# Half-turned keys and queries by transfers instead of matmuls, sums of squares in two parts, and four reorderings, in a two-block transformer kernel on one core

## The reference

```python
proj = einsum('btd,dn->btn', rmsnorm(h), w_in)
(gq, gk, gv, gz, gb, ga, aq, ak, av, iq, ik, iw, gate_a, gate_b) = split(proj)
# gated delta rule (GDN): q and k divided by their norms, per head of 128
q, k = _l2norm(q) * 128 ** -0.5, _l2norm(k)
# attention: 8 query heads aq, 2 key heads ak of 128, rotary position code
def _apply_rope(x, cos, sin):
    x1, x2 = x[..., :half], x[..., half:]
    return concatenate([x1 * c - x2 * s, x2 * c + x1 * s])
# index scores choose the keys that a query sees
s = einsum('bqhd,bsd->bqhs', qi, ki); s = einsum(relu(s), wi); top_k(s)
y_dsa = softmax(q k / sqrt(128), over the chosen keys) @ v
merged = sigmoid(gate_a) * (y_gdn @ w_a) + sigmoid(gate_b) * (y_dsa @ w_b)
```

## Time and profile before

| what | value |
|---|---|
| median of 3 runs | 1268.47 us (1268.13 to 1269.49) |
| profiled execution, its own time | 1269.95 us |
| its span | 1268.2 us |
| mean granted clock of PE | 0.998 |
| PE busy | 1254.3 us, 99% of the span |
| DVE, ACT, POOL busy | 919.6, 699.2, 154.3 us |

### The profile page before, as it was taken

How to read it: one execution, slowest core, us unless ns; L and a number is a source line. 1 busy time by engine, 2 the same in 40 slices (tenths; PEclk the granted TensorE clock), 3 DMA queues, 4 the chain that set the end, 5 groups by cost and what they waited for, 6 DMA issues and landing times.

```text
span 1268.2 us, 23324 instructions
## 1 busy us (share of the span) xinstructions
PE 1254.3 (99%) x9041; PEld 1169.6 (92%) x9041; DVE 919.6 (73%) x1290; ACT 699.2 (55%) x1082; POOL 154.3 (12%) x113
## 2 busy tenths in 40 slices
PE   9999999999999999999999999999999999999998
PEld 8997999999989998889998989999889998999986
DVE  6886874878778774447734547999758777999954
ACT  5556465654456343345354546666547567766642
POOL 0000142000000000000000001642200000464310
PEclk9999999999999999999999999999999999999999
DMA  7552332322355555555553444555564444454562
GB/s 300 189 173 101 133 134 101 133 68 68 152 197 188 195 179 185 198 170 182 183 209 109 156 173 167 198 169 195 194 221 171 162 154 163 167 188 175 197 224 93
DMA packets 30315, 212.83 MB, mean 168 GB/s; under 512 B 3488, under 2 KB 3616, under 8 KB 5152
## 3 DMA queue, kind: packets, MB, share of 16 engines
q1 hardware_dynamic: 29088, 206.53, 46.9%
q0 software_dynamic: 1152, 5.24, 1.1%
HBM read 210.71 MB, written 1.05 MB: 167 GB/s over the span
## 4 chain that ended last, share of the span: by engine, by line
PE 86%; DVE 8%; ACT 4%; DMA 1%; issue 1%; SPq 0%; DVEq 0%; ACTq 0%
PE lin L540 50%; PE lin L702 21%; DVE wlo L513 3%; PE lin L2883 2%; PE lin L567 2%; ACT whi L506 2%; PE lin L569 1%; DMA raw<-in_stream 1%; PE aux L2627 1%; PE aux L2599 1%; PE aux L2485 1%; ACT lm L1377 1%; PE aux L725 1%; PE aux L2745 1%; PE aux L2555 1%
## 5 line engine op out<-in xcount | busy, mean ns | idle before, releaser
L513 DVE TENSOR_TENSOR wlo<-raw,whi 128x2048 fp32r<-128x2048 f32 x183 | 427.4, 2338 | 170.8 <-ACT whi L506 170.1
L506 ACT CAST whi<-raw 128x2048 fp32r<-128x2048 f32 x192 | 365.3, 1906 | 179.5 <-DMA raw<-in_stream 147.0
L540 PE MATMUL lin<-xhi,whi 128*128 128x256 f32 (+2 forms) x1616 | 461.5, 286 | 1.0 <-DVE wlo L513 1.0
L540 PE MATMUL lin<-xlo,whi 128*128 128x256 f32 (+2 forms) x1616 | 457.0, 283 | 0.0
L540 PE MATMUL lin<-xhi,wlo 128*128 128x256 f32 (+2 forms) x1616 | 454.7, 281 | 0.0
L540 PEld LDWEIGHTS lin<-xhi,whi 128*128 128x128 f32 x1616 | 304.1, 188 | 3.0 <-DVE wlo L513 1.2
L540 PEld LDWEIGHTS lin<-xhi,wlo 128*128 128x128 f32 x1616 | 306.1, 189 | 0.0
L540 PEld LDWEIGHTS lin<-xlo,whi 128*128 128x128 f32 x1616 | 304.6, 189 | 0.4
L865 POOL TENSOR_TENSOR fu<-fs,ft 128x256 f32<-128x256 f32 x44 | 86.2, 1958 | 259.4 <-ACT fs L1479 259.4
L2292 DVE SCALAR_TENSOR_TENSOR ft<-fy,par,ft 128x254 f32<-128x254 f32 (+1 forms) x176 | 109.5, 661 | 5.9 <-DVE ft L2292 0.2
L540 PE MATMUL lin<-whi,xhi 128*128 128x256 f32 x256 | 74.2, 290 | 0.0
(11 more groups left out here) (454 smaller groups left out, 2123.2 us busy)
## 6 DMA issues: line engine op xcount, KB each, us to landing
raw<-in_stream SPq DMA_DIRECT2D x193, 1024.0 KB, 4.9
gp<-in_gains POOLq DMA_DIRECT2D x6, 512.0 KB, 3.9
c<-in_const SPq DMA_DIRECT2D x1, 1460.0 KB, 16.0
h<-in_x SPq DMA_DIRECT2D x2, 544.0 KB, 4.4
c<-in_const POOLq DMA_DIRECT2D x1, 1024.0 KB, 6.5
ht<-in_xtok POOLq DMA_DIRECT2D x1, 1024.0 KB, 9.6
out<-ht SPq DMA_DIRECT2D x1, 512.0 KB, 2.6
out<-ht SPq DMA_DIRECT2D x2, 256.0 KB, 2.0
```

The costliest lines, as they stand in the source:

```text
L506: nc.scalar.copy(whi[:, s0 % 4], raw[:, s0 % 4]).then_inc(hi_ready, 1)
L513: nc.vector.tensor_tensor(wlo[:, s0 % 4], raw[:, s0 % 4], whi[:, s0 % 4].bitcast(F32), ALU.subtract).then_inc(lo_ready, 1)
L540: ins = nc.tensor.matmul(out, a, b, start=start and n == 0, stop=stop and n == 2)
```

## The change

1. The matmuls that turned ak and aq go, and the constant `turna` with them. ACT waits for its own copy of ak or aq out of PSUM, then issues two transfers (`exchange`), one for each half of the partitions, that write the exchanged halves to new buffers `akr` and `aqr`: ten transfers of 64 partitions. The sign is now in the constant of the sines. DVE waits for both transfers (32) and does three operations as before, all from SBUF.
2. The table has another order. The sums of squares are cut into 5 and 11 matmuls with the index scores (0, 1) between; `sel` and `cum` come later, the decays' sums on DVE (`decay_sums`) go from `top(0)` into `top(1)`, two low halves on DVE come later. The second half of a tile's index scores uses the three banks that `l2sum` or `cum` doesn't hold. PE waits for rotations 7, 8 and 9 apart.
3. The cast of the third slot comes between the second and the third piece of `act_high_mix`.
4. Two parts of the branch projection (12 matmuls of 128 x 128) come ahead of a level of the GDN's first chunk; the decayed queries of the second chunk are made in two halves of four heads.
5. The very last tile is multiplied by its gains in one operation of 512 columns and gets two residuals of 512 in place of four pieces.

```diff
...
-PROJECT = [("rot", 0), ("iq", 0), ("iq", 1), ("rot", 1), ("rot", 2), ("av", 0), ("idx", 0, 0), ("lo", "aq", 1), ("l2", 0),
-           ("l2t", 0), ("sel", 0), ("idx", 0, 1), ("ak", 0), ("avt", 0), ("top", 0), ("cum", 0), ("idx", 1, 0), ("lo", "aq", 2), ("rot", 3), ("rot", 4),
+PROJECT = [("rot", 0), ("iq", 0), ("iq", 1), ("rot", 1), ("rot", 2), ("av", 0), ("idx", 0, 0), ("lo", "aq", 0),
+           ("l2", 0), ("idx", 0, 1), ("lo", "aq", 1), ("l2", 1), ("l2t", 0), ("ak", 0), ("avt", 0), ("top", 0),
+           ("sel", 0), ("idx", 1, 0), ("cum", 0), ("lo", "aq", 2), ("rot", 3), ("rot", 4),
...
-        ROT = ["rot_ik", "rot_iq0", "rot_iq1", "rot_ak0", "rot_ak1"] + [f"rot_aq{n}" for n in range(4)]
+        ROT = ["rot_ik", "rot_iq0", "rot_iq1"]
...
             if step[0] == "rot":
-                use_next(ROT[step[1]])
+                if step[1] < 3:
+                    use_next(ROT[step[1]])
+            elif step[0] == "idx" and step[2]:
+                others = [b for b in range(4) if b != USE[("l2sum", "cum")[step[1]]][0]]
+                for hh in range(4, 8):
+                    use(others[hh % 3], f"idx{step[1]}_{hh}")
...
                 use_next("avt0", "avt1")
-            elif step[0] in ("l2", "l2t", "sel", "cum"):
+            elif step[0] in ("l2t", "sel", "cum") or step == ("l2", 0):
                 use_next({"l2": "l2sum"}.get(step[0], step[0]))
-        use_next(ROT[8])
...
                 a = slice(n * 512, n * 512 + 512)
-                sp.wait_ge(S("h_postffn1"), 7 + 2 * n)
+                sp.wait_ge(S("h_postffn1"), 5 + n)
...
             for c in range(4):
+                if c == 2:
+                    load_hi(2, 0)
...
             act_high_mix(act)
-            load_hi(2, 0)
...
+            def exchange(dst, src, name):
...
+                for lo in (0, 64):
+                    act.dma_start(dst[lo:lo + 64], src[64 - lo:P - lo]).then_inc(S(name), 16)
...
                     nc.scalar.copy(ak[:], PS[u % 2][:, :, 0:T1]).then_inc(pair_free[u % 2], 1)
+                    pair_done(act, u)
+                    exchange(akr[:], ak[:], "swap_ak")
...
                     nc.scalar.copy(dst[:, 2 * j:2 * j + 2], PS[u % 2][:, :, META:T1]).then_inc(pair_free[u % 2], 1)
+                    if name == "aq":
+                        pair_done(act, u)
+                        exchange(aqr[:, 2 * j:2 * j + 2], aq[:, 2 * j:2 * j + 2], f"swap_aq{j}")
...
                     is_free(nc.scalar.copy(av[0:META, 2], b[0:META, 0:NCOL]), "avt1")
-                elif step[0] == "l2":
+                elif step[0] == "cum":
+                    act.wait_ge(S("bcg"), 1)
+                    own.link(nc.scalar.activation(kroot, knorm, ACT.Sqrt))
+                elif step == ("l2", 1):
...
                 elif step[0] in STEP_SLOTS:
-                    if step[0] == "ak":
-                        act.wait_ge(S("bcg"), 1)
-                        own.link(nc.scalar.activation(kroot, knorm, ACT.Sqrt))
...
             def second_tile(u):
+                if not pre:
+                    own.link(gained(u, 1, 0, 512, 512))
+                    dve.wait_ge(S("root_" + tag), 2)
+                    own.link(nc.vector.reciprocal(rc[:, 1:2], rc[:, 1:2]))
+                    residual(1, 0, 512)
+                    residual(1, 512, D)
+                    return
...
                 n = x.shape[1]
+                if step > 2:
+                    dve.wait_ge(S("swap_ak" if step < 5 else f"swap_aq{step - 5}"), 32)
+                    nc.vector.tensor_tensor(name, name, bc(cst(sn, lo=t0, n=W), n), ALU.mult)
+                    own.link(nc.vector.tensor_tensor(x, x, bc(cst(c, lo=t0, n=W), n), ALU.mult))
+                    nc.vector.tensor_tensor(x, x, name, ALU.add).then_inc(S("rope"), 1)
+                    dve.wait_ge(S("rope"), step + 1)
+                    return
...
             for step in PROJECT:
-                if step[0] == "iq":
-                    load_lo(FIRST["iq"] + step[1] + 3, 0)
+                if step == ("iq", 0):
+                    load_lo(FIRST["ak"], 0)
...
                 elif step[0] == "top":
-                    top_bias(step[1], between=None if step[1] else decay_sums)
+                    top_bias(step[1], between=decay_sums if step[1] else None)
...
                 own.link(nc.vector.tensor_tensor(dms[s][:, a], dms[s][:, a], gain, ALU.mult))
+                if between:
+                    between()
...
-            def decayed_queries(s):
-                q = qkv[:, 0:8, META + (s - 1) * P:META + s * P]
-                nc.vector.tensor_tensor(q, q, eg[:], ALU.mult).then_inc(S("ke"), 1)
+            def decayed_queries(s, h0, h1):
+                q = qkv[:, h0:h1, META + (s - 1) * P:META + s * P]
+                nc.vector.tensor_tensor(q, q, eg[:, h0:h1], ALU.mult).then_inc(S("ke"), 1)
...
             triangles(2, 0)
-            triangles(2, 1)
+            triangles(2, 1, lambda: decayed_queries(2, 0, 4))
...
             blocks(2)
+            decayed_queries(2, 4, H1)
             new_state(1)
-            decayed_queries(2)
-            dve.wait_ge(S("ke"), 2)
+            dve.wait_ge(S("ke"), 3)
...
             for n in range(2):
-                yield f"rot_ak{n}", ak[:, n:n + 1], T1, "cosa", "sina", 0
+                yield akr[:, n:n + 1], ak[:, n:n + 1], T1, "cosa", "sina", 0
             for n in range(4):
-                yield f"rot_aq{n}", aq[:, 2 * n:2 * n + 2], SEQ, "cosa", "sina", META
+                yield aqr[:, 2 * n:2 * n + 2], aq[:, 2 * n:2 * n + 2], SEQ, "cosa", "sina", META
...
                 name, x, W, c, sn, t0 = todo[step]
-                turn = cst("turni" if c == "cosi" else "turna")
+                turn = cst("turni")
...
                     pair_done(pe, 0)
-                elif name[:6] == "rot_iq":
+                else:
                     pair_done(pe, pair_first["iq"] + int(name[6:]))
-                elif name[:6] == "rot_ak":
-                    pair_done(pe, pair_first["ak"])
-                else:
-                    pair_done(pe, pair_first["aq"] + int(name[6:]))
...
                 if step[0] == "rot":
-                    rotation(step[1])
+                    if step[1] < 3:
+                        rotation(step[1])
...
                 elif step[0] == "l2":
-                    pe_head_sums(pe)
+                    pe_head_sums(pe, step[1])
...
                     project(step[0], step[1])
-            gate_part(0, 0, 2)
-            rotation(8)
-            gate_part(0, 2, 5)
-            pe.wait_ge(S("rope"), 9)
+            gate_part(0, 0, 5)
+            pe.wait_ge(S("rope"), 7)
...
             gate_part(0, 5, 6)
+            pe.wait_ge(S("rope"), 8)
...
             gate_part(0, 6, 7)
+            pe.wait_ge(S("rope"), 9)
...
             read_state(1, 1)
+            pe.wait_ge(S("slo"), 2)
+            branch(0, 0, 2)
...
                 additions(g)
-            pe.wait_ge(S("slo"), 2)
-            branch(0, 0, 3)
+            branch(0, 2, 3)
...
-        def pe_head_sums(pe):
...
-            b = fill("l2sum")
-            pe.wait_ge(S("l2sq"), 2)
-            for n in (*range(8, 16), *range(8)):
+        def pe_head_sums(pe, part):
...
+            if part == 0:
+                pe.wait_ge(S("l2sq"), 2)
+            b = AUX[USE["l2sum"][0]] if part else fill("l2sum")
+            for n in (*range(13, 16), *range(8)) if part else range(8, 13):
...
                 ins = nc.tensor.matmul(b[0:16, t0:T1], c1[:, a:a + 16], src[:, n % 8, t0:T1], start=n == 8, stop=n == 7)
-            is_full(ins, "l2sum")
+            if part:
+                is_full(ins, "l2sum")
...
```

More of the change, by code:

```diff
@@ L214, in program @@
         irelu = at("irelu", B + 74112, [P, 4, T1])
+        akr = at("akr", B + 67584, [P, 2, T1])
+        aqr = at("aqr", B + 82560, [P, 8, SEQ])
         zs = at("zs", B + 76288, [P, 8, SEQ])
@@ L3019, in constants @@
         c["cos" + tag], c["sin" + tag] = np.cos(ang), np.sin(ang)
-        turn = np.zeros((P, P), f)
-        for m in range(P):
-            lo = m % dim < dim // 2
-            turn[m + dim // 2 if lo else m - dim // 2, m] = -1.0 if lo else 1.0
-        c["turn" + tag] = turn
+    c["sina"] = np.where((i < 64)[:, None], -c["sina"], c["sina"])
+    c["turni"] = np.zeros((P, P), f)
+    for m in range(P):
+        lo = m % 64 < 32
+        c["turni"][m + 32 if lo else m - 32, m] = -1.0 if lo else 1.0
     past = [np.where(pos[None, :] <= (META + t * P + i)[:, None], 0.0, -BIG) for t in range(2)]
```

9 lines of the change are left out of this document (4 added, 5 removed).

## The result

The changed kernel takes 1277.32 us (median of 4 runs, 1275.17 to 1279.27), the kernel before in the same measurement 1268.3 (1267.64 to 1269.49): **slower by 0.7%, ratio 1.0071 with an interval of 1.0059 to 1.0083**. Forecast were 1265.2 us and a range up to 1268.2. The profiled execution is the fastest of the four: 1275.17 us, span 1273.0.

A forecast was written before the change was run, and what follows sets the result against it. PE, busy 99% of the span, was taken as the bound. Gains of 0.5 (attention, after the clock fall), 1.0 (start), 1.2 (GDN) and 0.45 (end) summed to 3.15, giving 1265.2 us; range 1262.4 to 1268.2.

The forecast's parts named there:

- the last exchange: Transfer for the last aq pair: assumed to land 3.0 us after its second issue, at 160.6, last rotation ending at 162.8.
- a late landing as a rival: Slower: last exchange lands after 9.6 us, attention loses 4.7, total 1270.5 us; deciding from a landing near 7.5. Chance 0.08.
- +1.9: Attention stage: last rotation's end, and what follows it, 1.9 us earlier if PE keeps its clock.
- I take 1.4: Slot aq 1, behind the new 3.0 us wait: a clock fall, held more likely than not, costing 1.4 us.
- the prediction's own signs of being wrong: Exchanges over 7 us, relu free without the cast ahead, or clock falling where the earlier trace shows none.
- the term of 1.75 us for the fall in `ak`: Slot ak: cutting the 16-column matmuls removes the clock fall, gaining 1.75 us; called the least certain gain, bounds 0 and 1.75.
- The start, GDN and end: Gains outside attention: 1.0 us from the third slot's cast, 1.2 from the branch matmuls, 0.45 from the last tile.
- The new wait of 3.0 us for ACT's relu: Behind aq 0: fourth matmul of index scores (1, 1) waits for its bank behind copy, issues, cast and relu; 3.0 us.
- the wait of 0.8 behind `ak`: Behind ak: ACT issues two transfers before copying avt out, so PE newly waits 0.8 us for banks.
- ACT is held for its issues as SP is: ACT's queue: 0.95 us taken for two issues with the copy's end, from SP's 0.90 for two; lower bound zero.
- Slot `ak` at 6.0: Slot ak takes 6.0 us at a clock of 1.00, in place of 7.76.
- the transfer and not DVE would be late next: Last rotation: DVE's own earliest end near 162.0, so the transfer is late next, by 0.8 us.

The follow-up runs named there:

- experiment 5: Changed kernel, but SP issues the weight slot freed by an ak or aq slot only once that slot's exchange has landed: 1273.29 us, ratio 1.0042.
- Experiment 6: Changed kernel with one transfer of 128 partitions in place of two of 64, halves not exchanged, so computation is left out: 1271.4 us, ratio 1.0032.
- Experiments 7: Changed kernel, but ACT casts the high part of the slot behind aq 0 after the relus of index scores (1, 1): 1272.4 us, ratio 1.0042.
- 9: Changed kernel plus 19 unread matmuls, 7 in the wait at index scores (1, 1) and 12 at the logits: 1272.76 us, ratio 1.0036.
- 10: Changed kernel plus only the 7 unread matmuls in the wait at index scores (1, 1): 1271.53 us, ratio 1.0033.
- 12: Kernel before with items 3, 4 and 5 of the change, plus three banks for index scores (1, 1), no exchange: 1269.01 us, ratio 1.0004.
- Experiment 15: Kernel before with items 3, 4 and 5, plus the sums of squares cut into 5 and 11 around index scores (0, 1): 1265.91 us, ratio 0.9984.
- experiments 8: Changed kernel, but the last pair of aq (rotation 9) is turned by a matmul as before: 1272.78 us, ratio 1.0026.
- 14: Kernel before with items 3, 4 and 5, plus the two DVE low halves moved behind the index scores: 1267.21 us, ratio 0.9992.
- 11: Changed kernel plus only the 12 unread matmuls in the wait at the logits: 1275.63 us, ratio 1.0057.

## Why the prediction was wrong

**The step that failed** is the last exchange, "I take 3.0, between 2.0 and 4.9, and nearer the row of the like size". It landed after 6.7 us, the others after 5.5 to 6.2. I went by the size; what counts is the weight slot issued within a us ahead of it (experiment 5). The row of the weight slot, 4.9, was taken as the upper bound and lies below every landing in the trace; the weight slots beside the exchanges took 5.8 themselves. Experiment 6 shows that even 256 KB take the same. That the two share the engines and the one issued second lands last is my reading of these rows. The prediction had a late landing as a rival, at a chance of 0.08. With the measured landing its own sum gives 4.88 - 6.7, or -1.8 us for the attention stage in place of +1.9, and with the other terms as they stand a kernel 0.5 us slower than before (-1.8 - 1.4 + 2.65), 1269 us. So this step alone does not explain the 1277.3.

Without a slot beside it the exchange took 2.2 to 2.4 us (experiment 5, the first two `aq` slots). The Trainium skill's page "DMA: Bandwidth & Descriptors", section "Anatomy of one DMA", gives a fit of 2.0 us and the bytes over 436 GB/s, for transfers that GpSimd issues; my estimate from it for these of ACT is 2.3 us. The trace agrees.

**The second failure, somewhat larger in us, is the price of an idle PE**: "I take 1.4", once. In the trace two stretches of about 7 us each cost 2.8 and 2.7 us of PE's work, and by their mean clocks the other executions lost more. My row showed a stretch of 3.4 us, and I carried its price over as if a fall had one length. Also I gave the wait at the logits, which the slower rival already held, no fall of its own; with 2.7 us for it the rival's point of decision would have been a landing of 4.8 us and not 7.5. Of the prediction's own signs of being wrong this one came: the clock fell behind the logits, where the trace of before shows no fall. ACT's copy of the last `aq` slot began at 160.22 in place of 156.5; the first stretch is 2.8 us of this. Experiments 7, 9, 10 and 12 show the mechanism: shortening or filling the waits raises the mean clock, and a wait added to a kernel without exchanges lowers it in six of eleven executions.

**The third** is the term of 1.75 us for the fall in `ak`. It was real in the profiled execution (1269.95 us, clock 0.998), and that is why that execution stands 1.5 us over the median. I had both numbers and still took the difference over to the median, where most executions have no such fall. Experiment 15 shows a gain of nothing. (The sum itself, 3.15 us below 1268.47, gives 1265.3 and not 1265.2.) An estimate of what the three come to, though they overlap on PE: 6.7 - 3.0 for the landing, 5.5 - 1.4 for the clock and 1.75, 9.5 us of the 12.1 between 1265.2 and 1277.3.

**What held.** The start, GDN and end: 2.65 forecast, 2.9 measured. The new wait of 3.0 us for ACT's relu: 3.1, by the mechanism told, and the wait of 0.8 behind `ak`: 0.7. ACT is held for its issues as SP is, 0.47 to 0.62 us each. Slot `ak` at 6.0: 6.2. A fall at the index scores' wait, though not its price. That the transfer and not DVE would be late next: yes, by 4.8 us and not 0.8. The rival that ended slower had the place right.

**What stays open.** Which executions fall, and for how long. The same kernel lies in two groups (experiments 8, 12 and 14), and in the traces of 8, 10 and 11 a fall comes behind short waits only, in slot `aq` 0, where the changed kernel's own trace has none. Its slower executions, at 0.992, may hold such a third stretch; no trace of one was taken. What is left of the 9.0 us beside the clock can't be split further: the late rotation, the waits and the falls overlap on PE.

## What to carry to other kernels

A transfer that is issued by the same event as a stream's next big block landed here with that block or behind it, small as it was; price it by the block, or let the block wait. Where PE is the bound, a new wait costs its length and often as much again in clock behind it: a wait of 1.7 us cost 2.3 us in some executions and 4 in others, and filling one of 3.1 us with spare matmuls was worth 5.8 us. And before a difference is credited to a row of one profiled execution, see whether that execution's own distance from the median is that very row.

## What the runs showed of the hardware

- An exchange of 128 KB within on-chip memory: 2.2 to 2.4 us from issue to landing without a weight slot beside it (2.6 the median of its kernel), 5.6 with one, 5.5 for 256 KB in one transfer; the weight slots of 1 MB beside the exchanges 5.8, the median of all of them 4.9.
- ACT's queue is held 0.47 to 0.62 us for each issue in the changed kernel.
- In PE waits of 3.1 and 5.3 us the granted clock went to the 1.2 GHz level 1.3 and 1.5 us ahead of the wait's end and stayed there for about 7 us each, although PE was busy again; in the kernel before the one such stretch lasted 3.4 us. In three traces a stretch of about 7 us came behind a wait of 0.7 us, in a fourth the same wait brought none.
- Mean clocks of whole executions, 0.992 to 1.000, go with most of the spread of one kernel's times: 1268.2 to 1269.1 us at 0.996 to 0.998 and 1272.6 to 1273.3 at 0.994 for one kernel, 1267.2 to 1267.6 at 0.999 or more and 1269.0 to 1269.4 at 0.997 or 0.998 for another.
